# Gram squares of 64 and 32 tokens in separate column groups of TensorE, in the gated linear attention of a two-stack transformer

## The chip, the cores and the metric

The kernel runs on one core of a Trainium2 chip. The time is device microseconds of one execution, as the median of several. Engines: PE is TensorE (matmuls, with its weight loads PEld), DVE is VectorE, ACT is ScalarE, SP is SyncE and only issues transfers here.

## The reference

Two stacks of two layers each run over 256 tokens of width 1024. The first has, in every layer, attention, a gated linear attention (GLA), a convolution and a feed-forward part, for a latent and for a context stream; the second stack is another transformer behind it. The change touches only the GLA scan, which runs in both directions, over 4 heads with keys of 128 channels and values of 256:

```python
def step(s, inp):
    qc, kc, vc, gc = inp
    b = jnp.cumsum(gc, axis=2)
    rel = jnp.where(lower, b[:, :, :, None, :] - b[:, :, None, :, :], -jnp.inf)
    a = jnp.einsum('bhid,bhjd,bhijd->bhij', qc, kc, jnp.exp(rel))
    o = jnp.einsum('bhid,bhde->bhie', qc * jnp.exp(b), s) + jnp.einsum('bhij,bhje->bhie', a, vc)
    ...
```

The weight of key j for query i is a sum over channels of q, k and a decay that depends on the channel and on both tokens.

## The kernel before, in words

All activations lie channels first (128 partitions) by tokens. Weights come as a stream of 723 loads of 512 KB. ACT rounds each load to its high part (`w_hi`, L1078), DVE takes the low part (`w_lo`, L1692), and a product `dense` is 24 matmuls of 128x256 for 8 tiles of weights (three for each tile, L489 to L491). PE, ACT and DVE each run an instruction list written out by hand, in order, and wait for one another through semaphores.

The first stack is four passes (layer by stream). Three of them are full ones and call `gla`: the context pass of layer 0 (here **the first pass**, its grams from 166 to 279 us), the latent pass of layer 0 (**the second**, 896 to 976 us) and the latent pass of layer 1 (**the third**, 1719 to 1798 us).

The kernel makes the 256x256 weights `A` without the chunks of the reference. It takes the pairs of tokens apart by level: for `half` in 128, 64, 32, 16, 8, 4, 2, 1 the tokens are cut into blocks of 2 x half, and a level holds the pairs with one token in the left half of a block and the other in its right half. The decay of such a pair splits at the middle of the block, so that `DL` can hold, for every token, k or q times its own part of the decay, and one matmul of `DL` with itself gives the products (the gram). Two directions make two steps for each level, 16 steps, and step 16 is the diagonal, made of `KG` and `QG` and added twice. So `STEPS` is 17, and for step j:

- DVE (`gla`, loop from L2037) first multiplies the decays of step j-1 with k and q (`decay`, L2017 and L2018, which raises `lev_ready`), then takes the differences of step j (`differences`, L2002/L2003 or L2007/L2008), then puts the gram of step j-2 into `A` (`place`: a copy for steps 0 and 1, for the others two copies under a mask, L2033, one for each half of the tokens), and then does what the interleaved units need, a `w_lo` above all. In steps 8 to 11 come four more passes over 1024 columns for the states (L1957 or L1966).
- ACT takes the exponential (L1366), evacuates the unit of PE and makes a `w_hi`.
- PE first runs the units that fill this step (a `dense` in each; in the first pass also, in most steps, `ada`, which is 16 matmuls with only two moving columns, L539, and in steps 13 to 16 the units of the states, L571 and L580), then waits for `lev_ready` of step j and for `a_copied` of step j-2, and makes the gram of step j: steps 0 and 1 at L733, 2 to 15 at L739, and the diagonal at L746, which waits for `a_copied` of step 14.

The grams of steps 2 to 15 are whole squares of 128 tokens, for 2 halves of the tokens and 4 heads, although the mask keeps only blocks of 2 x half on the diagonal of the square. Then, when all is placed, PE multiplies `A` with the values (L759, and L763 for the state). An fp32 matmul shows as two records in the trace, each with a weight load of its own, so that a step's 8 matmuls are 16 records. The fp32r matmuls of `dense` (L489 to L491) show as one record each.

L625, which the prediction reads, makes sums over channels for several heads: matmuls of 32 output columns and 256 moving ones, each head in another group of 32 columns of the array.

Of the kernel before, what the change touches and what calls it, by code (L numbers as in the profile page):

```python
# [28 lines left out]
P = 128  # L29
# [15 lines left out]
LEVELS = (128, 64, 32, 16, 8, 4, 2, 1)  # L45
# [29 lines left out]
GROUP, GROUPS = 32, P // 32  # L75
# [147 lines left out]
def program(nc, stream, first_in, rows_in, crow_in, ada_in, xt_in, cvec_in, vec1_in, vec2_in, glr_in, a2_in, const1_in, const2_in, small2_in, mask_in, out):  # L223
# [5 lines left out]
    with ExitStack() as ctx:  # L229
# [58 lines left out]
        KG = view(arena, 16 * S, GH, S)  # L288
        QG = view(arena, 20 * S, GH, S)
        VG = view(arena, 24 * S, QT, GH * GDV)  # L290
        Z = view(arena, 32 * S, 2 * GH, S)
        DL = view(arena, 32 * S, 2, GH, S)
# [159 lines left out]
        def _(pe):  # L452
# [265 lines left out]
            def gla(l, s):  # L718
                fill = gla_steps(l, s)
                a0 = n.at("a_copied")  # L720
                for j in range(STEPS):
                    for u in fill[j]:
                        unit(l, s, u)
                    pair = [aux[2 * (j % 2)], aux[2 * (j % 2) + 1]]
                    if j < STEPS - 1:
                        pe.wait_ge(sems["lev_ready"], at.up("lev_ready"))
                    if j >= 2:

                        pe.wait_ge(sems["a_copied"], a0 + j - 1)
                    if j < 2:  # L730
                        ks, qs = (0, P) if j == 0 else (P, 0)
                        for h in range(GH):
                            mm = pe.matmul(pair[0][:, h * P:(h + 1) * P], DL[:, j % 2, h, ks:ks + P],  # L733
                                           DL[:, j % 2, h, qs:qs + P], start=True, stop=True)
                    elif j < STEPS - 1:
                        for kt in range(QT):
                            for h in range(GH):
                                part = DL[:, j % 2, h, kt * P:(kt + 1) * P]
                                mm = pe.matmul(pair[kt][:, h * P:(h + 1) * P], part, part, start=True, stop=True)  # L739
                    else:  # L740

                        for kt in range(QT):
                            for h in range(GH):
                                tok = slice(kt * P, (kt + 1) * P)
                                for rep in range(2):
                                    mm = pe.matmul(pair[kt][:, h * P:(h + 1) * P], KG[:, h, tok], QG[:, h, tok],  # L746
                                                   start=rep == 0, stop=rep == 1)
                    mm.then_inc(sems["gram_done"], 1)
                n.up("a_copied", STEPS)
                if s == LAT:  # L750
                    pe.wait_ge(sems["hat_ready"], at.up("hat_ready", 2))

                pe.wait_ge(sems["a_copied"], n.at("a_copied"))
                for h in range(GH):
                    o = bank()
                    for c in range(2):
                        e = h * GDV + c * P
                        for kt in range(QT):
                            mm = pe.matmul(o[:, c * S:(c + 1) * S], VG[:, kt, e:e + P], A[:, h, kt, :],  # L759
                                           start=kt == 0, stop=kt == QT - 1 and s == CTX)  # L760
                        if s == LAT:
                            for d in range(2):
                                mm = pe.matmul(o[:, c * S:(c + 1) * S], state[:, d, h, c * P:(c + 1) * P],  # L763
                                               HAT[:, h, d, :], start=False, stop=d == 1)
                    done(mm)
# [207 lines left out]
            for l in range(DEPTH):  # L973
# [31 lines left out]
                for tt in range(QT):  # L1005
                    mm = pe.matmul(o[:, tt * MH * MV:(tt + 1) * MH * MV], w2["ckv"][:, 0, tt * P:(tt + 1) * P], vcols,
                                   start=True, stop=True)
# [1642 lines left out]
```

## Time and profile before

| | |
|---|---|
| median of 3 runs | 3044.44 us (3039.38 to 3047.6) |
| the profiled execution | 3033.33 us, span 3031.6 us |
| granted TensorE clock, mean | 0.955 |
| PE / PEld busy | 94% / 90% of the span |
| DVE / ACT busy | 73% / 50% |
| HBM read | 447 MB, 148 GB/s |

The profiled execution is one run and took 11.1 us less than the median of the others. The span runs from its first to its last instruction. PE's busy share is that of overlapping records; how close PE is to its limit is read from the distance between starts.

### The profile page before, as it was taken

Reading aid. Unit: us, or ns where it says so; the run is one execution under the profiler, and the core shown is the slowest. Engines: PE = TensorE matmul, PEld = TensorE weight load, DVE = VectorE, ACT = ScalarE, POOL = GpSimd, SP = SyncE. Lnnn points to the kernel's source line nnn. Section 1 sums busy time; section 2 is a strip of 40 time slices with the busy share of each in tenths; the row PEclk is TensorE's granted clock in tenths of the full one; section 3 lists DMA queues with packets and bytes.
Section 4 is the critical chain, followed back from the end, with each engine's and each line's share of the span. In section 5 each row is a group of like instructions: output and inputs, shape, how many; then the busy total and the mean of one; then the engine's idle time right before and its main releaser. Section 6 shows DMA issues by size and latency. Waiting matters only on the chain.

```text
span 3031.6 us, 54592 instructions
## 1 busy us (share of the span) xinstructions
PE 2838.8 (94%) x21440; PEld 2716.1 (90%) x21440; DVE 2204.4 (73%) x3798; ACT 1514.1 (50%) x3111; POOL 0.2 (0%) x4
## 2 busy tenths in 40 slices
PE   8999999999999999999989998999999889997998
PEld 7999889899989889889989997888998779995998
DVE  6976777678889876867767898867666665566655
ACT  3644345454565335445564653454555455555554
POOL 0000000000000000000000000000000000000000
PEclk7999999999999989989999999999999899998999
DMA  7542444456742333447733423335553325541554
GB/s 265 157 160 94 146 133 153 152 176 222 232 137 91 105 124 127 143 169 236 232 117 118 143 76 118 111 125 179 166 183 117 105 81 187 185 140 52 160 185 153
DMA packets 123335, 451.45 MB, mean 149 GB/s; under 512 B 13744, under 2 KB 15792, under 8 KB 122464
## 3 DMA queue, kind: packets, MB, share of 16 engines
q1 hardware_dynamic: 108704, 393.30, 40.2%
q10 hardware_dynamic: 14400, 54.86, 5.3%
q8 instruction: 171, 2.80, 0.4%
q14 instruction: 60, 0.49, 0.1%
HBM read 447.05 MB, written 1.05 MB: 148 GB/s over the span
## 4 chain that ended last, share of the span: by engine, by line
PE 65%; DVE 22%; ACT 6%; DMA 4%; issue 2%; SPq 0%; ACTq 0%; DVEq 0%
PE lin L489 15%; PE lin L490 15%; PE lin L491 15%; DVE arena L1869 5%; DVE w_lo L1692 5%; DMA w_raw<-in_stream 3%; PE lin L539 3%; PE aux L604 2%; ACT w_hi L1078 2%; PE aux L739 1%; DVE rstd L1717 1%; PE aux L651 1%; PE aux L672 1%; PE aux L595 1%; PE lin L517 1%
## 5 line engine op out<-in xcount | busy, mean ns | idle before, releaser
L1692 DVE TENSOR_TENSOR w_lo<-w_raw,w_hi 128x1024 fp32r<-128x1024 f32 x722 | 875.2, 1220 | 321.3 <-ACT w_hi L1078 314.9
L489 PE MATMUL lin<-h_hi,w_hi 128*128 128x256 f32 x3456 | 997.3, 289 | 5.2 <-ACT arena L1346 2.9
L1078 ACT ACTIVATE w_hi<-w_raw 128x512 fp32r<-128x512 f32 x1446 | 828.7, 623 | 323.8 <-DMA w_raw<-in_stream 232.8
L490 PE MATMUL lin<-h_lo,w_hi 128*128 128x256 f32 x3456 | 985.7, 285 | 0.0
L491 PE MATMUL lin<-h_hi,w_lo 128*128 128x256 f32 x3456 | 985.4, 285 | 0.0
L489 PEld LDWEIGHTS lin<-h_hi,w_hi 128*128 128x128 f32 x3456 | 672.2, 195 | 9.9 <-ACT arena L1346 4.9
L490 PEld LDWEIGHTS lin<-h_lo,w_hi 128*128 128x128 f32 x3456 | 671.9, 194 | 0.5
L491 PEld LDWEIGHTS lin<-h_hi,w_lo 128*128 128x128 f32 x3456 | 671.1, 194 | 0.0
L489 PE MATMUL lin<-s_hi,w_hi 128*128 128x256 f32 x1520 | 450.6, 296 | 26.6 <-DVE s_lo L1778 23.2
L490 PE MATMUL lin<-s_lo,w_hi 128*128 128x256 f32 x1520 | 441.0, 290 | 0.0
L491 PE MATMUL lin<-s_hi,w_lo 128*128 128x256 f32 x1520 | 440.0, 289 | 0.0
L489 PEld LDWEIGHTS lin<-s_hi,w_hi 128*128 128x128 f32 x1520 | 302.4, 199 | 36.2 <-DVE s_lo L1778 28.0
L490 PEld LDWEIGHTS lin<-s_lo,w_hi 128*128 128x128 f32 x1520 | 303.2, 199 | 1.1 <-issue 0.5
L491 PEld LDWEIGHTS lin<-s_hi,w_lo 128*128 128x128 f32 x1520 | 302.9, 199 | 0.0
L1869 DVE SCALAR_TENSOR_TENSOR arena<-arena,vec 128x256 f32<-128x256 f32 x720 | 290.2, 475 | 0.0
L1795 DVE SCALAR_TENSOR_TENSOR X<-X,gate_buf 128x256 f32<-128x256 f32 x120 | 50.9, 425 | 142.1 <-ACT gate_buf L1238 56.9
L539 PEld LDWEIGHTS lin<-cvec,a_raw 128*128 128x128 f32 x928 | 116.5, 202 | 11.5 <-DMA a_raw<-in_ada 8.9
L539 PE MATMUL lin<-cvec,a_raw 128*128 128x2 f32 x928 | 114.5, 254 | 7.1 <-DMA a_raw<-in_ada 7.0
L1717 DVE RECIPROCAL rstd<-std 128x256 f32<-128x256 f32 (+1 forms) x34 | 59.5, 1751 | 83.8 <-ACT std L1107 83.8
L1224 ACT ACTIVATE gate_buf<-lin 128x256 f32<-128x256 f32 x110 | 41.7, 379 | 102.6 <-PE lin L491 86.3
L517 PE MATMUL lin<-w_hi,h_hi 128*128 128x256 f32 x320 | 90.8, 284 | 1.5 <-ACT arena L1313 1.5
L519 PE MATMUL lin<-w_lo,h_hi 128*128 128x256 f32 x320 | 90.6, 283 | 0.0
(278 smaller groups left out, 3858.9 us busy)
## 6 DMA issues: line engine op xcount, KB each, us to landing
w_raw<-in_stream SPq DMA_DIRECT2D x723, 512.0 KB, 3.5
a_raw<-in_ada ACTq DMA_DIRECT2D x58, 512.0 KB, 3.4
arena<-in_rows ACTq DMA_DIRECT2D x38, 512.0 KB, 5.1
arena<-in_first SPq DMA_DIRECT2D x2, 2048.0 KB, 19.6
X<-in_tokens SPq DMA_DIRECT2D x2, 1024.0 KB, 14.6
s_f<-in_ada SPq DMA_DIRECT2D x4, 512.0 KB, 10.3
arena<-in_ada SPq DMA_DIRECT2D x4, 512.0 KB, 17.2
arena<-in_const ACTq DMA_DIRECT2D x1, 1856.0 KB, 7.9
```

What stands on the lines that cost most here:

```text
L489: used(pe.matmul(o, whi, hi[:, k, :], start=k == 0, stop=False), first)
L490: pe.matmul(o, whi, lo[:, k, :], start=False, stop=False)
L491: mm = pe.matmul(o, wlo, hi[:, k, :], start=False, stop=k == kcs - 1)
L517: mm = pe.matmul(o[:, 0:2 * P], xhi, whi, start=k == 0, stop=False)
L519: pe.matmul(o[:, 0:2 * P], xhi, wlo, start=False, stop=False)
L539: mm = pe.matmul(o[:, 0:2], w[:, k, :], cvec[:, k, :], start=k == 0, stop=k == KC - 1)
L604: mm = pe.matmul(aux[1][:, 0:S], c1("mean1024"), squares[:, k, :], start=k == 0, stop=k == KC - 1)
L1078: act.activation(w_hi[:, slot, part], w_raw[:, raw, part], ACT.Copy).then_inc(sems["hi_ready"], 1)
L1692: dve.tensor_tensor(w_lo[:, m % SLOTS, :], w_raw[:, m % RAW, :], w_hi[:, m % SLOTS, :].bitcast(F32), ALU.subtract).then_inc(sems["lo_ready ...
L1717: step(dve.reciprocal(r, std[0:rows, slot, :]))
L1795: dve.scalar_tensor_tensor(x[:, c, :], x[:, c, :], alpha, gate_buf[:, c % 2, :], ALU.mult, ALU.add).then_inc(sems["r_ready"], 1)
L1869: dve.scalar_tensor_tensor(CV[:, c, :], YP[:, c, tap:tap + S], v1(l, "conv_w", c * TAPS + tap), CV[:, c, :], ALU.mult, ALU.add).then_inc(s ...
```

## The change

In steps 4 to 15 (levels 32 to 1) each square of 128 tokens is replaced by the squares on its diagonal: two of 64 tokens for level 32, four of 32 tokens for the levels below. A square of tokens b to b+w is written to partitions b to b+w of PSUM, so that the squares of one head lie in different column groups of PE. The diagonal, too, is made in squares of 32 tokens. The rest of the 128x128 area in PSUM is no longer written; the mask leaves it out, as before. Steps 0 to 3 stay.

```diff
                     elif j < STEPS - 1:
+                        w = max(2 * LEVELS[j // 2], GROUP)
                         for kt in range(QT):
                             for h in range(GH):
-                                part = DL[:, j % 2, h, kt * P:(kt + 1) * P]
-                                mm = pe.matmul(pair[kt][:, h * P:(h + 1) * P], part, part, start=True, stop=True)
+                                for b in range(0, P, w):
+                                    part = DL[:, j % 2, h, kt * P + b:kt * P + b + w]
+                                    mm = pe.matmul(pair[kt][b:b + w, h * P + b:h * P + b + w], part, part, start=True, stop=True)
                     else:
 
                         for kt in range(QT):
                             for h in range(GH):
-                                tok = slice(kt * P, (kt + 1) * P)
                                 for rep in range(2):
-                                    mm = pe.matmul(pair[kt][:, h * P:(h + 1) * P], KG[:, h, tok], QG[:, h, tok],
-                                                   start=rep == 0, stop=rep == 1)
+                                    for b in range(0, P, GROUP):
+                                        tok = slice(kt * P + b, kt * P + b + GROUP)
+                                        mm = pe.matmul(pair[kt][b:b + GROUP, h * P + b:h * P + b + GROUP], KG[:, h, tok], QG[:, h, tok],
+                                                       start=rep == 0, stop=rep == 1)
```

`P` is 128, `GROUP` 32, `QT` 2 halves of the tokens, `GH` 4 heads. The count of matmuls goes from 8 to 16 in steps 4 and 5, from 8 to 32 in steps 6 to 15, and from 16 to 64 in the diagonal. No other engine's list changes.

On PE at the end of the first pass's grams, steps 15 and 16 (L739, now L741, is the gram of a step; L571 and L580 belong to the states, L539 is `ada`), the difference is:

```order
 L491 MATMUL lin<-h_hi,w_lo 128x256
 L571 MATMUL lin<-const,s_f 128x128 x8
-L739 MATMUL aux<-arena 128x128 x8
+L741 MATMUL aux<-arena 32x32 x32
 L539 MATMUL lin<-cvec,a_raw 128x2 x8
 L580 MATMUL lin<-arena,s_f 128x256 x8
-L746 MATMUL aux<-arena 128x128 x16
-L759 MATMUL lin<-arena 128x256 x16
+L749 MATMUL aux<-arena 32x32 x64
+L762 MATMUL lin<-arena 128x256 x16
 L489 MATMUL lin<-h_hi,w_hi 128x256
```

Nothing moves past anything else: each gram stands where it stood, in more and smaller pieces (L759 and L762 are the same line).

On PE at the end of the second pass's grams, before:

```order
L491 MATMUL lin<-h_hi,w_lo 128x256
L739 MATMUL aux<-arena 128x128 x8
L746 MATMUL aux<-arena 128x128 x16
L759 MATMUL lin<-arena 128x256 x2
L763 MATMUL lin<-s_f,arena 128x256 x2
```

and now:

```order
L491 MATMUL lin<-h_hi,w_lo 128x256
L741 MATMUL aux<-arena 32x32 x32
L749 MATMUL aux<-arena 32x32 x64
L762 MATMUL lin<-arena 128x256 x2
L766 MATMUL lin<-s_f,arena 128x256 x2
```

Here the gram of step 15 and the diagonal follow each other with no unit between them: 24 matmuls have become 96.

## Rows read from the trace of the kernel before

**Rows 1.** page, part 1 (busy us, share of the span, instructions) and part 4 (chain)
```profile
PE 2838.8 (94%) x21440; PEld 2716.1 (90%) x21440; DVE 2204.4 (73%) x3798; ACT 1514.1 (50%) x3111; POOL 0.2 (0%) x4
...
PE 65%; DVE 22%; ACT 6%; DMA 4%; issue 2%; SPq 0%; ACTq 0%; DVEq 0%
```

**Rows 2.** groups of matmuls on PE: line, shape, count | busy us, mean ns | idle
```profile
L739 PE MATMUL aux<-arena 128*128 128x128 f32 x672 | 85.8, 282 | 4.7 <-DVE arena L2018 4.7
...
L746 PE MATMUL aux<-arena 128*128 128x128 f32 x96 | 11.2, 275 | 0.0
```

**Rows 3.** timeline, PE, one step of the first pass: start us, us, instructions, xcount
```profile
203.41 1.84 PE L539 MATMUL lin<-cvec,a_raw 128*128 128x2 f32 x16
205.11 2.03 PE L739 MATMUL aux<-arena 128*128 128x128 f32 x16
206.90 0.36 PE L489 MATMUL lin<-h_hi,w_hi 128*128 128x256 f32 x1
207.10 0.28 PE L490 MATMUL lin<-h_lo,w_hi 128*128 128x256 f32 x1
...
211.56 0.47 PE L739 MATMUL aux<-arena 128*128 128x128 f32 x2
```

**Rows 4.** timeline, PE, around four column groups in use (L625)
```profile
300.14 0.28 PE L490 MATMUL lin<-h_lo,w_hi 128*128 128x256 f32 x1
300.26 0.28 PE L491 MATMUL lin<-h_hi,w_lo 128*128 128x256 f32 x1
300.47 1.07 PE L625 MATMUL aux<-arena,const 128*32 128x256 f32 x16
301.47 0.39 PE L489 MATMUL lin<-h_hi,w_hi 128*128 128x256 f32 x1
301.69 0.28 PE L490 MATMUL lin<-h_lo,w_hi 128*128 128x256 f32 x1
```

**Rows 5.** instructions of L625 up to 300.6 us: first and last start
```profile
L625 PE MATMUL aux<-arena,const x4: 403/403/404, 300.5 to 300.5; 128*32 128x256 f32 x4
```

**Rows 6.** timeline, PE, the same shape over all 128 columns (L595)
```profile
1259.18 3.62 PE L595 MATMUL aux<-X,const 128*128 128x256 f32 x16
```

**Rows 7.** timeline, DVE, the decays that release the gram at 211.56
```profile
207.37 0.68 DVE L2018 TENSOR_TENSOR arena<-arena 128x512 f32<-128x512 f32 x1
```

**Rows 8.** busy us by stretch: PE, PEld, DVE, ACT, POOL, PEclk, DMA share, GB/s
```profile
220.00:235.00 15.00, 15.00 (x134) 15.00 (x132) 15.00 (x22) 7.20 (x14) 0.00 (x0) 1.00 0.55 175
905.00:965.00 60.00, 57.81 (x487) 56.85 (x486) 60.00 (x89) 30.59 (x50) 0.00 (x0) 1.00 0.33 106
```

**Rows 9.** timeline, DVE, one step of the second pass, from w_lo to w_lo
```profile
962.78 1.20 DVE L1692 TENSOR_TENSOR w_lo<-w_raw,w_hi 128x1024 fp32r<-128x1024 f32 x1
...
967.55 1.20 DVE L1692 TENSOR_TENSOR w_lo<-w_raw,w_hi 128x1024 fp32r<-128x1024 f32 x1
```

**Rows 10.** timeline, DVE, end of the second pass's grams
```profile
969.89 1.33 DVE L2033 COPY_PREDICATED arena<-masks,aux 128x512 f32<-128x512 uint8 x2
...
975.68 1.33 DVE L2033 COPY_PREDICATED arena<-masks,aux 128x512 f32<-128x512 uint8 x2 [2.22 <-PE aux L746]
```

**Rows 11.** timeline, PE, the same stretch
```profile
970.02 2.05 PE L739 MATMUL aux<-arena 128*128 128x128 f32 x16
971.91 3.74 PE L746 MATMUL aux<-arena 128*128 128x128 f32 x32
977.11 1.10 PE L759 MATMUL lin<-arena 128*128 128x256 f32 x4 [1.47 <-issue]
```

**Rows 12.** timeline, PE, first pass, a gram at the lower clock
```profile
188.42 1.84 PE L539 MATMUL lin<-cvec,a_raw 128*128 128x2 f32 x16
190.58 3.51 PE L739 MATMUL aux<-arena 128*128 128x128 f32 x16 [0.32 <-DVE arena L2018]
```

**Rows 13.** busy us by stretch, same columns as rows 8
```profile
190.90:194.30 3.40, 3.40 (x18) 3.40 (x17) 3.40 (x6) 1.06 (x1) 0.00 (x0) 0.50 0.44 157
```

**Rows 14.** page, part 3: the queue that fetches instructions
```profile
q8 instruction: 171, 2.80, 0.4%
```

## The prediction

> **What bounds the kernel now.** The page comes first: PE is busy 94% of the span and is 65% of the chain of waits, with DVE 22% [rows 1]. So work taken from PE counts, unless DVE stands right behind it. The groups of PE then say how large the edited part is: 672 records at L739 and 96 at L746 [rows 2], that is 14 steps of 16 and one of 32 in each of three passes. In the timeline of the first pass one gram runs from 205.11 to the next product at 206.90, 1.79 us for 16 records, 112 ns each [rows 3]. The edited part (12 steps and a diagonal of 3.57 us) is 25 us in a pass and 75 us in all. That is the most that could go.
>
> Whether it goes is read from the two kinds of passes. In the first, PE has `ada` beside `dense`, a step is 211.56 - 205.11 = 6.45 us [rows 3], and PE is the bound. In the second the table of busy time shows DVE busy 60.00 of 60 us while it makes the steps [rows 8], and DVE goes from one `w_lo` to the next in 967.55 - 962.78 = 4.77 us [rows 9]. There a faster gram only makes PE wait. The third pass repeats the second.
>
> **The price of a small square.** The trace has one place where groups of 32 columns are used in turn, L625. Its first four records start together [rows 5], and 16 records with 256 moving columns take 301.47 - 300.47 = 1.00 us [rows 4]. The same 16 records over all 128 columns take about 3.3 us, from 1259.18 to about 1262.45 (3.62 us to the modelled end less some 0.35) [rows 6]. So four column groups stream at once, a round of four in about 0.215 us. With 32 moving columns a round should take 32/256 of that, 27 ns; a step of 64 records is 16 rounds, 0.43 us. That is the lower bound. The upper bound is no overlap at all: 32 moving columns for each of 64 records, a quarter of 112 ns each, 1.79 us. I take **0.65 us**, near the lower end because the row shows the overlap, half as much again because no row shows weights of 32 columns renewed every 27 ns. For 64 tokens, two groups at once, 32 records are 16 rounds of 54 ns, 0.86 us; I take 0.90 (upper bound 1.79). For the diagonal, 32 rounds, 0.86 us; I take 1.3 (upper bound 3.57).
>
> **The price of changing over.** Into L625 the distance of starts is 300.47 - 300.26 = 0.21 instead of 0.12 us, and out of it 301.69 - 301.47 = 0.22 after 1.00 us of which the four rounds are 0.86 [rows 4]. Out of today's gram it is 207.10 - 206.90 = 0.20 [rows 3]. Going in costs 0.09 and coming out 0.14 + 0.02, so 0.25 us for each step. The Trainium skill, "TensorEngine Tiling (Array Packing)", Key Properties, says that a change of tiling mode drains the engine; by that rule, the trace agrees, with this 0.25 us.
>
> **First pass.** Steps 6 to 15: 1.79 - 0.25 - 0.65 = 0.89 us less, ten times, -8.9. Steps 4 and 5: 1.79 - 0.25 - 0.90 = 0.64, twice, -1.3. The diagonal: 3.57 - 0.25 - 1.3 = 2.0, -2.0. Together -12.2 us on PE.
>
> Three things give some of it back. DVE: its step is 4.8 us, and steps 8 to 11 each hold one more operation of about 1.1 us, 23.8 us for the four. PE would need 6.45 - 0.89 = 5.6 us for a step with `ada` and 3.9 for step 8, which has none (`ada` takes 205.11 - 203.41 = 1.70 [rows 3]), 20.7. DVE is already busy 15.00 of 15 us there [rows 8]. It has slack, since the decays for the gram at 211.56 ended at about 207.97 [rows 7], 3.6 us early, some 2.7 with the faster PE. The stretch and step 12, again without `ada`, use that up, and I put back 1.3 us. The clock: I allow for one more stretch at half clock than now, +1.7 us (below). Lost cover for the states' units (they wait for ACT with the gram as filler): within these. Sum of the first pass: **-9.2 us**.
>
> **Second and third pass.** In the steps nothing, hidden by DVE. The end differs: the last gram starts when its decays are ready, at 970.02, the diagonal at 971.91 [rows 11], and DVE, done with step 14 at about 971.2, waits for PE twice and places the diagonal at 975.68 [rows 10]. Now the gram of step 15 ends by 970.9, the diagonal may start once step 14 is placed, at 971.2, and takes 1.3 us and the changeover; with the 0.3 us from last start to DVE's start, the place comes at 972.9, 2.8 us earlier. Step 15 is placed meanwhile. A x V at 977.11 [rows 11] follows. ACT has activations of its own to finish first and cannot evacuate 2.8 us earlier, but four banks are free. Twice -2.8, of which I take off 0.6 for a colder start of A x V: **-5.0 us**.
>
> **Sum.** -14.2 us, on the profiled execution's 3033.3 a time of 3019. That execution lies 11 us under the median, so I set the change against the median: 3044.4 - 14.2 = 3030.2 us. DVE, ACT and the transfers get no work. Instructions grow by 608 matmuls and weight loads each in a pass, 3,648 in all; the queue that fetches them moves 2.80 MB in 0.4% of the DMA time today [rows 14], about 65 bytes for each of PE's 42,880, and gets 8% more. I cost that at nothing.
>
> **Rivals.**
>
> *The pieces cost by the record, not by their columns (0.12).* If small records don't overlap, a step is 1.79 + 0.25 us, 0.25 more than now. Twelve steps and the diagonal give +3 us in the first pass; in the others only the end grows, by 0.5 each. Then the time is 3044.4 + 4 = 3048. Against it speaks the common start of four records [rows 5]; for it, that those had 256 columns to stream. The Trainium skill speaks for it: the same page, Instruction Overhead, gives each matmul about 60 cycles and warns against tiling a dimension that is already small, as the moving one is here. At 2.4 GHz that would be 25 ns a record, 1.6 us for 64, 1.85 with the changeover, and no gain; no row here has such short records in different column groups.
>
> *The clock falls more often (0.18).* In the first pass the gram behind an `ada` began at 190.58 and took 3.51 us [rows 12], since the granted clock was 0.50, the 1.2 GHz level, from 190.9 to 194.3 [rows 13]. Before it PE had run 16 matmuls of two moving columns and then waited 0.32 us for DVE [rows 12]. The smaller gram lengthens each such thin stretch. A stretch of 3.4 us at half clock costs 1.7. If five of the eleven steps with `ada` bring one, four more than I allow, that is +6.8, and one at each end of the latent passes another +3: 3040 us. For it speaks that each step then has 2.9 us of dense work in 5.6; against it, that four groups streaming at once are not idle.
>
> *PE starves for instructions (0.14): the slower side.* A step of the second pass would issue 128 records for the gram (64 matmuls, 64 loads) and 48 for the `dense`, 176 in 4.78 us, and 208 in the first pass in 5.6. So the supply has to deliver one each 27 ns; there it decides. The trace shows 32 in 1.00 us (31 ns) only in a short burst [rows 4], and over long stretches 112 ns for a pair, 56 each [rows 3]. At 35 ns a step of the latent passes becomes 6.2 us, +1.4 ten times, and the diagonal 9.0, +5.4: +19 in each, +15 in the first pass, +54 in all, 3098 us. At 56 ns it is +195, 3239. Against it: PE is paced by the array in those stretches (112 ns for 128 columns twice), so they only bound the supply from one side.
>
> **How the numbers follow.** Forecast 0.53, the rivals 0.12, 0.18 and 0.14, and 0.03 that all goes better (lower bounds for every square, nothing given back, 3023). A difference of 0.3%, 9 us, is about what a measurement of this kernel can tell from none: faster ends at 3035.3, slower starts at 3053.6. The forecast lies below the first almost wholly, the clock's rival one time in three: faster 0.58. Most of the clock's rival, the rival by the record and a little of the forecast are within: 0.26. Starvation and the ends of the others: 0.16. The range takes in the first three cases with some 4 us for the median's scatter, 3018 to 3050, and leaves starvation out.
>
> **What would show it.** Records of a 32-token step starting within 0.5 to 0.8 us from first to last, four to a round; a distance of about 5.6 us between grams in the first pass where it was 6.45, unchanged 4.77 in the second, with PE now waiting for DVE (L2018) about 1 us before each gram; the diagonal placed some 2.8 us sooner after the last decays. Wrong would be: first-to-last over 1.5 us (by the record or starved, the latter if `dense` behind it slows too), or PEclk under 1.00 in the stretches from 195 to 270 us.

## The result, and the profile after

| | before | changed |
|---|---|---|
| median | 3041.58 us (7 runs, 3033.29 to 3056.62) | 3025.88 us (7 runs, 3022.54 to 3032.68) |
| ratio | | 0.9947, interval 0.9924 to 0.997 |
| the profiled execution | 3033.33 us | 3023.83 us, span 3022.1 us |
| mean granted clock | 0.955 | 0.952 |

The change saves 15.7 us by the medians, where 14.2 were forecast. The profiled executions differ by only 9.5 us, since that of the kernel before lies 8.2 us under its median; this is why the forecast was set against the median.

The page of the changed kernel, in the order of [rows 1] and [rows 14]:

```profile
PE 2807.6 (93%) x23264; PEld 2677.2 (89%) x23264; DVE 2203.6 (73%) x3798; ACT 1512.8 (50%) x3111; POOL 0.2 (0%) x4
...
q8 instruction: 185, 3.03, 0.4%
...
PE 61%; DVE 24%; DMA 6%; ACT 6%; issue 3%; SPq 0%; ACTq 0%; DVEq 0%
```

PE has 31 us less to do, which is more than the time fell, and part of the chain has gone from PE to DVE and to "issue". The groups of PE with shapes kept apart (busy us, mean ns | idle before), to be held against [rows 2]:

```profile
L741 PE MATMUL aux<-arena 128*32 128x32 f32 x1920 | 23.2, 200 | 20.9 <-DVE arena L2021 20.9
L741 PE MATMUL aux<-arena 128*64 128x64 f32 x192 | 7.5, 237 | 0.3 <-DVE arena L2021 0.3
L749 PE MATMUL aux<-arena 128*32 128x32 f32 x384 | 4.1, 198 | 2.8 <-issue 1.9 <-DVE arena L2036 1.0
```

The idle time before the 32-token grams, 20.9 us, is new (all grams of steps 2 to 15 had 4.7 [rows 2]): PE now waits for DVE's decays (L2021, which was L2018), and nearly all of it lies in the two latent passes. The timeline of PE in the first pass answers to [rows 3]:

```profile
205.10 1.84 PE L539 MATMUL lin<-cvec,a_raw 128*128 128x2 f32 x16
206.87 0.76 PE L741 MATMUL aux<-arena 128*32 128x32 f32 x64
207.56 0.39 PE L489 MATMUL lin<-h_hi,w_hi 128*128 128x256 f32 x1
207.79 0.28 PE L490 MATMUL lin<-h_lo,w_hi 128*128 128x256 f32 x1
...
210.63 0.76 PE L741 MATMUL aux<-arena 128*32 128x32 f32 x64
```

From the first record of the gram to the next product it is 207.56 - 206.87 = 0.69 us (1.79 before). The 64 starts lie within 0.57 us, in rounds of four that, but for the first, are 32 ns apart. The step behind it, without `ada`, is 210.63 - 206.87 = 3.76 us (4.74 before); those with `ada` are 5.45, 5.67 and 5.92 us (5.6 forecast, 6.45 before). In the second pass the same view shows the other case, and at its end something that was not foreseen:

```profile
956.67 0.77 PE L741 MATMUL aux<-arena 128*32 128x32 f32 x64 [0.96 <-DVE arena L2021]
957.36 0.39 PE L489 MATMUL lin<-h_hi,w_hi 128*128 128x256 f32 x1
...
961.45 0.77 PE L741 MATMUL aux<-arena 128*32 128x32 f32 x64 [0.96 <-DVE arena L2021]
962.72 1.28 PE L749 MATMUL aux<-arena 128*32 128x32 f32 x127 [0.50 <-DVE arena L2036]
965.85 0.22 PE L749 MATMUL aux<-arena 128*32 128x32 f32 x1 [1.85 <-issue]
967.54 2.05 PE L762 MATMUL lin<-arena 128*128 128x256 f32 x4 [1.47 <-DVE arena L2036]
```

The distance of steps stays at 961.45 - 956.67 = 4.78 us, that of DVE in [rows 9], and PE waits 0.96 us in each. The diagonal's 128 records would be through in 1.1 us, but 127 of them run and then PE stands for 1.85 us, and the profile shows no engine that releases it ("issue"). The third pass has no such stop (same view):

```profile
1786.69 0.76 PE L741 MATMUL aux<-arena 128*32 128x32 f32 x64 [0.93 <-DVE arena L2021]
1787.95 1.30 PE L749 MATMUL aux<-arena 128*32 128x32 f32 x128 [0.50 <-DVE arena L2036]
1790.92 1.10 PE L762 MATMUL lin<-arena 128*128 128x256 f32 x4 [1.67 <-issue]
```

From the last gram to A x V it took 7.09 us before [rows 11]; now it is 6.09 in the second pass and 4.23 in the third. Behind the stop, A x V itself is slower. The first `dense` record after it, in the kernel before:

```profile
990.82 0.47 PE L489 MATMUL lin<-h_hi,w_hi 128*128 128x256 f32 x1
```

and in the changed kernel:

```profile
984.24 0.47 PE L489 MATMUL lin<-h_hi,w_hi 128*128 128x256 f32 x1
```

That is 990.82 - 977.11 = 13.7 us before and 984.24 - 967.54 = 16.7 us now. Busy time by stretch (columns as in [rows 8]) for the two stretches of [rows 8], and three short ones, the last in A x V:

```profile
220.00:235.00 15.00, 14.59 (x287) 14.17 (x285) 15.00 (x22) 7.31 (x14) 0.00 (x0) 0.89 0.57 177
905.00:965.00 60.00, 48.29 (x1113) 45.26 (x1111) 59.03 (x88) 33.08 (x51) 0.00 (x0) 0.97 0.33 107
222.70:226.10 3.40, 3.40 (x45) 3.34 (x35) 3.40 (x6) 1.06 (x1) 0.00 (x0) 0.50 0.54 161
942.90:946.30 3.40, 3.40 (x35) 3.34 (x22) 3.40 (x5) 1.06 (x1) 0.00 (x0) 0.50 0.02 5
966.80:973.60 6.80, 6.06 (x14) 4.88 (x15) 6.80 (x18) 3.09 (x3) 0.00 (x0) 0.50 0.01 2
```

PE's busy time in the 60 us of the second pass fell from 57.81 to 48.29 with nothing gained there, and both stretches now hold time at the lower clock, 1.2 GHz, where both had 1.00.

What a stretch at half clock costs depends on where it falls. The one at 942.9 falls where DVE is the bound:

```profile
942.31 0.80 PE L741 MATMUL aux<-arena 128*32 128x32 f32 x64 [2.08 <-DVE arena L2021]
947.53 0.76 PE L741 MATMUL aux<-arena 128*32 128x32 f32 x64
951.88 0.76 PE L741 MATMUL aux<-arena 128*32 128x32 f32 x64 [0.52 <-DVE arena L2021]
```

The step that holds it takes 5.22 us and the next one 4.35, together 9.57, which is two steps of DVE's 4.78. PE made up the loss out of its own waits: the stretch cost no time. Nor did the one at 1762.1 in the third pass (steps of 4.80 us), nor the one at 222.7 in the first, where the gram behind it starts at 232.92 and DVE's decays for it end at 232.86. Where PE is the bound it does cost: 3.0 us for the 6.8 us in A x V, and 1.5 us for a stretch at 253.4 in the first pass (a step of 7.92 us, which is 6.43 in e6_fill below, where no such stretch falls in it).

From the first gram to the first `dense` behind A x V, the second pass took 94.99 us before and takes 96.62 now; the third took 94.20 and takes 91.40.

### The profile page after: what moved, and what is told of

Its sections match the earlier page's. It is cut to its first block, busy times and chain, and to the rows that moved or that the text cites. A ratio compares the mean times of both kernels' runs of the same rounds, so it can differ in the third digit from the quotient of the medians.

```text
span 3022.1 us, 58240 instructions
## 1 busy us (share of the span) xinstructions
PE 2807.6 (93%) x23264; PEld 2677.2 (89%) x23264; DVE 2203.6 (73%) x3798; ACT 1512.8 (50%) x3111; POOL 0.2 (0%) x4
## 3 DMA queue, kind: packets, MB, share of 16 engines
q8 instruction: 185, 3.03, 0.4%
## 4 chain that ended last, share of the span: by engine, by line
PE 61%; DVE 24%; DMA 6%; ACT 6%; issue 3%; SPq 0%; ACTq 0%; DVEq 0%
PE lin L489 14%; PE lin L490 14%; PE lin L491 14%; DVE w_lo L1695 5%; DVE arena L1872 5%; DMA w_raw<-in_stream 4%; PE lin L539 2%; ACT w_hi L1081 2%; PE aux L604 2%; DVE rstd L1720 1%; DVE arena L2036 1%; PE aux L651 1%; PE aux L672 1%; DMA a_raw<-in_ada 1%; PE aux L595 1%
## 5 line engine op out<-in xcount | busy, mean ns | idle before, releaser
L539 PEld LDWEIGHTS lin<-cvec,a_raw 128*128 128x128 f32 x928 | 116.5, 202 | 13.5 <-DMA a_raw<-in_ada 10.7
L539 PE MATMUL lin<-cvec,a_raw 128*128 128x2 f32 x928 | 115.0, 255 | 8.8 <-DMA a_raw<-in_ada 8.8
```

The costliest lines, as they stand in the source:

```text
L539: mm = pe.matmul(o[:, 0:2], w[:, k, :], cvec[:, k, :], start=k == 0, stop=k == KC - 1)
```

## Experiments

Twelve kernels ran, each beside runs of the kernel before on the same chip. Two figures help beyond the median. Every run has its span and its mean granted clock c. The time at half clock is 2(1 - c) times the span, and **span times c** is the length the run would have if PE's work alone filled it and the clock never fell. Where PE waits for DVE that condition fails: a stretch of 3.4 us at half clock as at 942.9 lengthens nothing, but takes 1.7 us off span times c. Such a stretch is called free below. Single runs of the kernel before have a standard deviation of about 5 us in the span and 4 in span times c. Means over the runs, with their standard errors (e3_one_group, e5_group_major and e13_shifted ran once each and stand in their own sections):

| kernel | runs | median us | ratio, interval | span x c | at half clock |
|---|---|---|---|---|---|
| before (beside e1, e2, e3, e5) | 18 | 3038.70 | | 2895.6 ± 0.7 | 284 ± 3 |
| changed, as above | 7 | 3025.88 | 0.9947, 0.9924 to 0.997 | 2876.7 ± 1.1 | 297 ± 5 |
| e1_context | 7 | 3029.63 | 0.9958, 0.994 to 0.9977 | 2882.8 ± 1.4 | 290 ± 4 |
| e2_latent | 12 | 3043.18 | 1.0008, 0.9991 to 1.0024 | 2889.4 ± 1.0 | 302 ± 4 |
| before (beside e6, e7) | 17 | 3038.13 | | 2895.6 ± 0.9 | 282 ± 3 |
| e6_fill | 6 | 3019.34 | 0.9942, 0.9929 to 0.9955 | 2881.5 ± 1.5 | 273 ± 4 |
| e7_whole_less_dve | 10 | 3034.16 | 0.999, 0.9974 to 1.0006 | 2891.0 ± 0.8 | 286 ± 4 |
| e7_small_less_dve | 4 | 3010.86 | 0.9908, 0.989 to 0.9926 | 2866.7 ± 3.0 | 284 ± 7 |
| before (beside e9 to e12) | 26 | 3040.63 | | 2895.5 ± 0.8 | 287 ± 2 |
| e9_latent_fill | 12 | 3031.83 | 0.9972, 0.9959 to 0.9985 | 2888.0 ± 1.0 | 284 ± 4 |
| e10_fill_from_6 | 6 | 3021.71 | 0.9936, 0.9915 to 0.9956 | 2878.0 ± 0.5 | 285 ± 4 |
| e11_changed_again | 9 | 3018.86 | 0.9937, 0.9918 to 0.9957 | 2874.2 ± 0.9 | 292 ± 5 |
| e12_before_fill | 12 | 3038.26 | 0.9997, 0.9985 to 1.0009 | 2894.1 ± 0.9 | 287 ± 3 |

### Where the gain is made: the first pass, or the latent ones

Small squares in the context pass alone, or in the latent passes alone (`s == LAT`):

```diff
-                        w = max(2 * LEVELS[j // 2], GROUP)
+                        w = max(2 * LEVELS[j // 2], GROUP) if s == CTX else P
...
+                                w = GROUP if s == CTX else P
-                                    for b in range(0, P, GROUP):
+                                    for b in range(0, P, w):
```

> Small squares only in the first (context) pass, whole squares in the two latent passes. Theory A (PE bounds the first pass, DVE the steps of the latent ones): the first pass is as short as with the whole change, 104 to 106 us from its first gram to A x V instead of 114.2, and the time is 9 to 12 us below the kernel before, about two thirds of the change. Rival B (the gain is spread evenly over the three passes): 5 us below. Rival C (the half-clock stretches that small squares bring cost more in the latent passes than their ends give): at or below the time of the whole change, 14 us or more under the kernel before.

> Small squares only in the two latent passes. Theory A: the steps stay at 4.77 to 4.9 us and the diagonal is placed 2.8 us sooner, so each latent pass is 1.4 to 3 us shorter from first gram to A x V, and the time is 3 to 6 us below the kernel before. Rival B (evenly spread): 10 us below. Rival C: no gain or slower, because A x V starts at half clock (the changed kernel's profile has it so in the second pass) and loses 3 us behind the grams.

The first has a ratio of 0.9958, 9.1 us less by the medians and 12.8 by span times c, 11.1 without the free stretch that its first pass has like the changed kernel's. Its first pass takes 106.09 us to A x V, 0.1 above what theory A allows, with 3.4 us more at half clock in it than the changed kernel has there. So theory A holds and the larger part of the gain is made here.

The second has 1.0008, where theory A expected 3 to 6 us less. Within the passes theory A holds: they take 79.74 and 78.40 us to A x V where the kernel before has 81.29 and 80.50. By span times c it saved 6.2 us. It also spent 18 ± 5 us more at half clock, and the mean span is 2.7 ± 2.0 us longer. The two savings by span times c, 12.8 and 6.2, add up to 19.0, and the changed kernel has 18.9 and, in its second set of runs, 21.3.

Two stretches of the latent passes' half clock in e2_latent (columns as above), the second in A x V:

```profile
947.10:950.50 3.40, 3.40 (x67) 3.34 (x54) 3.40 (x6) 1.06 (x1) 0.00 (x0) 0.50 0.07 28
977.80:981.20 3.40, 3.05 (x7) 2.52 (x8) 3.40 (x10) 2.51 (x3) 0.00 (x0) 0.50 0.02 5
```

The first is free: the step that holds it takes 5.90 us, and 5.91 in the kernel before. So is one at 1773.1. The second costs 1.5 us: A x V takes 15.23 us to the first `dense` behind it instead of 13.70. Without the two free ones, span times c gives the latent passes 2.8 us and not 6.2. To that `dense` the second pass takes 94.97 us, nothing gained on 94.99, because the stop and the slow A x V take back what the end of the grams gives; the third takes 92.10 after 94.20. Why the mean of the whole kernel is not some 2 us shorter, as these passes are, the runs don't show.

### What makes a small square cheap: one column group, or a poor order

All squares written to partitions 0 up, so that they share one column group; the weights `A` are then incomplete:

```diff
-                                    mm = pe.matmul(pair[kt][b:b + w, h * P + b:h * P + b + w], part, part, start=True, stop=True)
+                                    mm = pe.matmul(pair[kt][0:w, h * P + b:h * P + b + w], part, part, start=True, stop=True)
```

The diagonal, too, goes to partitions 0 to 31, and its two additions to a square follow each other directly.

> The small squares all go to partitions 0 up, so to the same column group of PE, one behind the other; the rest of the squares is left out of the result. Theory A (the column groups work side by side): 64 records of 32 columns take 64 times 27 ns, 1.7 us, from first to last start instead of 0.57, the 32 records of 64 columns the same, the diagonal 3.4, and the first pass is as long as before or up to 4 us longer (114 to 118 us). Rival D (small squares are cheap because they are small, or because records are issued every 8 ns whatever group they go to): 0.57 us again, first pass 105 us.

And the same squares, where they belong, but in steps 4 to 15 all squares of a column group first, then those of the next:

```diff
-                        for kt in range(QT):
-                            for h in range(GH):
-                                for b in range(0, P, w):
+                        for b in range(0, P, w):
+                            for kt in range(QT):
+                                for h in range(GH):
```

> The same squares, but all eight of one column group first, then all of the next, so that neighbours in the instruction list share a group (steps 4 to 15; the diagonal stays). Theory A1 (PE starts records in the order of the list, apart from waiting for its group): no overlap but at the borders, 64 records take 1.6 to 1.75 us. Theory A2 (a record that waits for its group lets those for other groups past): with enough records looked at ahead it stays at 0.6 to 0.9 us. First pass 105 us under A2, 113 to 116 under A1.

Timeline of PE, first pass, of the kernel with one column group:

```profile
204.85 1.84 PE L539 MATMUL lin<-cvec,a_raw 128*128 128x2 f32 x16
206.63 2.21 PE L741 MATMUL aux<-arena 128*32 128x32 f32 x64
208.77 0.39 PE L489 MATMUL lin<-h_hi,w_hi 128*128 128x256 f32 x1
```

and of the one in order of groups:

```profile
208.03 1.91 PE L741 MATMUL aux<-arena 128*32 128x32 f32 x64
```

With one group a gram takes 208.77 - 206.63 = 2.14 us, more than the whole squares' 1.79: its records start 32 ns apart. In order of groups the 64 starts span 1.72 us; they are 32 ns apart too, and only some 6 records at each border between groups overlap. In the changed kernel the same 64 take 0.57. The squares are the same in all three; what differs is that in the changed kernel each matmul goes to another column group than the one ahead of it. The first pass takes 127.32 us to A x V with one group, more than the 114 to 118 expected: a record took 32 ns and not 27, and 27 us of the pass were at half clock, where the kernel before has 10. In order of groups it takes 116.24, as theory A1 has it. Executions: 3054.60 and 3043.11 us, one run each, beside a median of 3038.70: neither is a gain.

### What bounds the latent steps

DVE puts only the first half of each gram of steps 2 to 16 into `A` in the latent passes, in the kernel before (whole squares) and in the changed one (small squares). The other half of `A` is left out.

```diff
-                    for kt in range(QT):
+                    for kt in range(QT if s == CTX else 1):
                         ins = dve.copy_predicated(A[:, :, kt, kt * P:(kt + 1) * P], over(masks[:, j - 2, :], GH),
```

> The kernel before (whole squares), but in the latent passes DVE puts only one half of each gram of steps 2 to 16 into A: the other half of A is left out, and DVE has 0.66 us less in each step. Theory D (the latent steps of the changed kernel are bound by DVE, those of the kernel before by PE and DVE almost equally): here PE is the bound, 4.66 to 4.75 us a step, as the first pass's steps without ada have 4.74; hat steps fall from 5.9 to about 5.3. Rival E (something else paces the steps, such as the loads or the chain of ACT's exponential): 4.77 as before.

> The changed kernel (small squares) with the same part left out: DVE puts only one half of each gram of steps 2 to 16 into A in the latent passes. Theory D: the bound moves to DVE at 4.1 to 4.2 us a step (PE needs 3.8), so ten steps and the end give some 6 to 8 us a pass, and this kernel is 12 to 18 us faster in the latent passes than the one with whole squares and the same part left out, on top of the 10 to 13 us of the first pass: ratio to before 0.985 to 0.990. Rival E: the steps stay at 4.7 to 4.8 and the gap between the two kernels is that of the changed kernel and the one before, 16 us.

PE's timeline late in the second pass, the kernel before (the next gram is at 970.02 [rows 11]):

```profile
965.24 2.05 PE L739 MATMUL aux<-arena 128*128 128x128 f32 x16
```

whole squares with less work on DVE:

```profile
961.45 1.95 PE L739 MATMUL aux<-arena 128*128 128x128 f32 x16
966.11 1.95 PE L739 MATMUL aux<-arena 128*128 128x128 f32 x16
```

and small ones with less work on DVE:

```profile
948.81 0.76 PE L741 MATMUL aux<-arena 128*32 128x32 f32 x64 [0.33 <-DVE arena L2021]
952.98 0.76 PE L741 MATMUL aux<-arena 128*32 128x32 f32 x64 [0.34 <-DVE arena L2021]
```

The late steps of the kernel before take 4.78 us, at DVE's pace. With 0.66 us less on DVE the whole squares take 4.66, only 0.12 less, and PE waits for nothing: that is PE's own bound. (The kernel before has 4.66 as well between its grams at 910.88 and 929.52, while DVE, which is ahead there, goes on at 4.78.) With small squares the step falls to 4.17, and even then PE waits for DVE. So theory D holds for the steps. In sum: from first gram to A x V the small squares save 5.5 and 8.9 us in the two latent passes of this pair (78.21 to 72.73, 79.00 to 70.11), where the changed kernel saves 1.4 and 2.8. The pair differs by 23 us in the medians (3034.16 and 3010.86); at least 22 were expected. The ratio of 0.9908 lies just outside the 0.985 to 0.990 expected, and the second pass of this kernel has a stop too, as below.

### Is it given back at the lower clock

PE's waits in the latent passes are filled with useless matmuls, ahead of the wait for `lev_ready` and ahead of the one before A x V:

```diff
+                    if s == LAT and 4 <= j < STEPS - 1:
+                        pe.wait_ge(sems["a_copied"], a0 + j - 1)
+                        for _ in range(4 if j in (10, 11) else 2):
+                            pe.matmul(pair[0][:, 0:S], c1("mean1024"), const1[:, 0:S], start=True, stop=True)
...
+                    if s == LAT and h == 0:
+                        for _ in range(4):
+                            pe.matmul(o[:, 0:S], c1("mean1024"), const1[:, 0:S], start=True, stop=True)
```

> The changed kernel, with PE's waits of the two latent passes filled: before each gram of steps 4 to 15 it runs 2 matmuls of 128x256 (4 in steps 10 and 11) into the PSUM area that the gram then overwrites, and 4 before A x V, all of them useless. Each shows as 2 records of 0.216 us, 0.43 us in all. Theory G (in the latent passes the smaller squares did gain 1.4 to 2.8 us a pass, and it is given back because PE's new waits of 1 us bring more stretches at half clock): distances of steps stay at 4.79, no stretch at half clock inside the latent gram passes (the changed kernel has four, at 942.9, 966.8, 1714.3 and 1762.1), A x V 6 us behind the last gram at full clock, time about 3021, ratio to before 0.992 to 0.994. Rival H (stretches at half clock come from elsewhere, or the total is set by their chance places): the time stays at the changed kernel's 3026, ratio 0.995. Rival I (the filling is itself in the way): distances of steps over 4.9 and a time of 3030 or more.

> Small squares in the two latent passes only, as in e2_latent, with PE's waits filled from step 6 on (2 useless matmuls of 128x256 before each gram, 4 in steps 10 and 11, 4 before A x V). Steps 4 and 5, where the filling of e6_fill lengthened steps of 4.75 and 4.19 us to 5.62 and 5.02, are left alone. Theory G (the 1.5 to 2.8 us gained in each latent pass are given back by stretches at half clock that PE's new waits bring): ratio to before 0.998 to 0.999, -3 to -6 us, where e2_latent had 1.0008; no half-clock stretch within the latent gram passes. Rival H (what is gained there is lost by chance elsewhere, or was never gained): ratio as e2_latent's, 1.000 to 1.001.

> The changed kernel with the same filling, in the latent passes from step 6 on. Theory G: 1.5 us faster than e6_fill for the steps 4 and 5, 3 to 6 us faster than the changed kernel, that is 3016 to 3020 where the kernel before has 3038; ratio 0.9935 to 0.994. Rival H: as the changed kernel's run beside it.

> The changed kernel once more, on the same chip as the filled ones: ratio to before 0.9947 with some 0.001 to either side; half the half-clock time above e10_fill_from_6 is what the filling saves.

> The kernel before (whole squares), filled where it has waits in the latent passes: 2 useless matmuls in steps 10 and 11, 3 before A x V. Theory G: little to win, because whole squares leave PE no waits in the other steps and its latent passes hold no half-clock stretch: ratio 0.999 to 1.000. Rival J (filling before A x V helps any version): ratio 0.998 or less, and then the gain of the filled kernels is no return of what the small squares lost.

Ten us of the second pass in the changed kernel (columns as above):

```profile
938.00:948.00 10.00, 7.92 (x161) 7.51 (x161) 10.00 (x15) 3.48 (x7) 0.00 (x0) 0.83 0.27 77
```

and with the filling, e6_fill:

```profile
938.00:948.00 10.00, 9.90 (x188) 8.93 (x187) 10.00 (x15) 3.83 (x6) 0.00 (x0) 1.00 0.22 81
```

In the latent passes' grams of the filled kernels' profiles no half clock is left but the one at the first gram, which the kernel before has too (e10_fill_from_6 has one more, at its A x V). For small squares in the latent passes alone, filling turns 1.0008 into 0.9972, and the intervals don't meet (the two ran on different chips, each against the kernel before on its own): the time at half clock falls from 302 to 284 us, that of the kernel before. The kernel before gains nothing by it (0.9997), so rival J falls. The filling is worth something in that pair, more than the 3 to 6 us that theory G expected. But the cause that theory G gives is not shown: the half clock that went from the steps had been free. The profiles place 3.5 us of the gain in the two passes (94.97 to 92.07 and 92.10 to 91.47 us, to the first `dense` behind A x V), most of it the stop of the next section and the slow A x V behind it, which e9_latent_fill doesn't have. Where the rest was gained is open.

For the changed kernel the total is as rival H has it: 0.9936 filled and 0.9937 not. Span times c is 3.8 us longer with the filling, and free stretches explain it: e11_changed_again has two in its latent steps (942.3 and 1761.5) and e10_fill_from_6 none, which makes 3.4 us of difference in span times c and none in time. e6_fill (0.9942, the upper edge of what theory G expected) is 4.8 us longer by this figure than the first set of the changed kernel: 3.4 for the free stretches and 3.4 for its filled steps 4 and 5 (5.62 and 5.02 us where they had 4.75 and 4.19, 1.7 in each pass), less 1.9 for the stop that it doesn't have. No version is shown to beat the changed kernel.

### The stop before the last record of the diagonal

The 1.85 us stop recurs before the same record in e11_changed_again, e7_small_less_dve and (1.33 us) e5_group_major, and elsewhere inside the diagonal of e2_latent and e10_fill_from_6, always in the second pass; e6_fill and e9_latent_fill have none. Traffic of the changed kernel's queues from 963.0 to 964.7 us (packets, MB, share):

```profile
q8 instruction: 1, 0.02, 4.5%
```

One block of instructions (3.03 MB in 185 packets is 16.4 KB each) is being fetched; it starts at 963.39, ends at 964.61, and PE goes on at 965.85. In all six the fetch starts between 0.9 us ahead of the last record that PE still starts and 0.1 us after it, and PE goes on 1.2 to 1.4 us after it has ended. To move the place where a block ends, 50 matmuls of 32x32 were added in the waits of steps 14 and 15 (j = 13 and 14) of the second pass:

```diff
+                    if l == 0 and s == LAT and j in (13, 14):
+                        pe.wait_ge(sems["a_copied"], a0 + j - 1)
+                        for k in range(25):
+                            b = k % 4 * GROUP
+                            pe.matmul(pair[0][b:b + GROUP, b:b + GROUP], const1[:, 0:GROUP], const1[:, 0:GROUP], start=True, stop=True)
```

> The changed kernel with 50 useless matmuls of 32x32 (100 records and 100 weight loads) in PE's waits of steps 14 and 15 of the second pass alone, so that the place where the instruction queue's next block of 16 KB is needed falls some 200 instructions away. Theory K (the 1.85 us for which PE stood still before the last record of the second pass's diagonal, with an instruction fetch under way, is one block of instructions that came too late, because the last gram and the diagonal use more than a block's worth in 3 us): no stall inside the diagonal, from the first record of the last gram to A x V 4.2 us as in the third pass, where the changed kernel had 6.09 in the second. Rival L (something at this place of the program holds PE, such as ACT's table load or the placing of the last gram): 6.1 us again. The time itself cannot show it.

Timeline of PE:

```profile
959.95 0.76 PE L746 MATMUL aux<-arena 128*32 128x32 f32 x64 [0.96 <-DVE arena L2026]
961.22 1.30 PE L754 MATMUL aux<-arena 128*32 128x32 f32 x128 [0.50 <-DVE arena L2041]
964.17 1.10 PE L767 MATMUL lin<-arena 128*128 128x256 f32 x4 [1.66 <-issue]
```

All 128 records run, and A x V comes 4.22 us behind the last gram instead of 6.09. The block's fetch now starts at 962.33, when the diagonal's last record starts, and falls into PE's wait for A x V. Rival L falls, since the place in the program is the same. That the useless matmuls also fill two waits is not the reason either: e10_fill_from_6 has those waits filled and stops all the same. So theory K holds: the stop is an instruction block that comes too late. Each kernel shows it in one profiled execution (two for the changed squares).

What follows the stop costs time as well. The five kernels that stood for 1.8 to 2.2 us all have half clock in the A x V right behind it (from 966.8, 966.2, 977.8, 961.8 and 967.3 us), e5_group_major with 1.33 us has none there, and no latent pass without a stop has any. In e13_shifted the second pass takes 91.45 us from its first gram to the first `dense` behind A x V, where the changed kernel takes 96.62: 1.9 of the 5.2 us are the stop, 3.0 the slow A x V, 0.3 lie at the first gram. One execution of each is compared here, two of the changed kernel (96.62 and 96.76). (The run took 3015.67 us and the kernel before beside it 3033.80, with 271 and 273 us at half clock; one run each, too few to show 5 us in the time.)

## Why the prediction was right, and where it was not

**The bound.** As forecast: in the latent passes DVE takes 4.77 us a step and PE's own step is only 0.1 us shorter, and PE was the bound in the first pass. Both e7 kernels show the one, e1_context the other.

**Price of a small square.** 0.57 us for the burst of 32-token squares (0.65 forecast), 0.93 for the 64-token ones (0.90), 1.10 for the diagonal (1.3). Changing over: 0.69 - 0.57 = 0.12 us from the last start, then 207.79 - 207.56 = 0.23 for the first product instead of 0.12, and 0.09 going in: with the burst 0.89 us for a gram (0.90 forecast). One term was missed: the whole square, too, had 0.20 instead of 0.12 behind it [rows 3], so that a step saves 0.98 and not 0.89. Ten steps without that 0.09 are 0.9 us too few.

**First pass.** -9.2 us forecast; from its first gram to A x V it is 104.62 us after 114.21, -9.6. The mechanism is right and three sizes were off, in part against each other. PE saved an estimated 13.3 and not 12.2: 0.98 us ten times, and 0.2 more in the diagonal. The steps that DVE paces gave back the rest, about 2.2, where 1.3 was put; steps 8 to 11 come at DVE's 5.9 us each, as the forecast's 23.8 us for four has it. The clock took 1.5 us (the stretch at 253.4) where 1.7 was allowed.

**Latent passes.** -5.0 us forecast, twice -2.8 less 0.6 for a cold A x V. To A x V the third pass is as forecast, 7.09 - 4.23 = 2.86 us, and to the first `dense` behind it 94.20 - 91.40 = 2.8. The second lost what it gained and is 96.62 - 94.99 = 1.6 us longer: 1.9 us went into the stop and 3.0 into the A x V at half clock behind it. Together -1.2 us where -5.0 were forecast. The steps at fault are "I cost that at nothing", of the instructions, and the 0.6 us allowed for the cold A x V, which measured 3.0. "In the steps nothing, hidden by DVE" holds: the new waits cost nothing, and the half clock that came with them was free.

**The sum.** The passes of the profiled execution are 9.6 + 1.2 = 10.8 us shorter and not 14.2. By the medians the change is worth 15.7 us in the first set of runs and 22 in the second (18.7 ± 2.6 by the mean spans). Span times c gives 19 and 21 us; three free stretches (222.7, 942.9, 1762.1), if they fall in every execution as in both profiled ones, account for 5.1 of that, and 14 to 16 us are left. The passes of the profile, less what the clock cost in them (1.5 and 3.0), give 15.3. So 14 to 16 us is the worth of the change at full clock; the forecast has 16.5 for it, its terms without the 1.7 and 0.6 for the clock. That the first median lies within 1.5 us of the forecast is partly luck: the latent passes gave 4 us less than forecast, and the clock's scatter, some 12 us in the time at half clock of a single run and so 6 in its time, is as large as such an error.

**The rivals.** *By the record*: fell. It needs 1.79 us for 64 records; they took 0.57, 9 ns each. It is right where the squares share a column group, or come in the order of groups: 32 ns a record. The Trainium skill, "TensorEngine Tiling (Array Packing)", Instruction Overhead, gives about 60 cycles for each matmul, an estimate of 25 ns at 2.4 GHz: the traces come near it in one column group (32 ns) and not over four in turn (9 ns). *The clock falls more often*: half right. Its sign came, PEclk 0.89 in 220:235, and the changed kernel's profile has five more stretches in the gram passes than before (222.7, 253.4, 942.9, 1762.1, and 966.8 in A x V). But three of them were free, and the other two cost 1.5 and 3.0 us: 2.2 beyond the 2.3 allowed, where the rival named 9.8. *Starved of instructions*: as a steady rate it fell. 128 instructions in 0.57 us are 4.5 ns each, where it needed 27 to decide. As an event it was real, once in a run: 1.9 us long, and with the half clock behind it 4.9. The forecast's nothing looked at the queue's mean traffic [rows 14], not at the 384 instructions of the last gram and the diagonal, which use up one and a half blocks (of some 250) in 2.4 us.

## What to carry to other kernels

Cut a block-diagonal matmul into squares on separate column groups, and write the list so that each matmul goes to another group than the one ahead of it; in the order of groups the pieces cost as much as the whole. Before counting what PE saves, see how far the next engine is behind in each stage. Look also at what the many small instructions draw from the instruction queue in the densest burst, not on average. A fall of the clock is priced by the stage it falls in: where another engine sets the pace, compare the distances of steps before and after, since it may cost nothing. In a kernel whose clock changes by chance, compare span times mean clock as well as the median, but take off the free stretches first: here they made 5 of 19 to 21 us.

## What the runs showed of the hardware

- fp32 records of 32 weight columns and 32 moving columns start 32 ns apart while they stay in one column group, and about 9 ns apart on average over four groups in turn. A following record of another group starts early only if it is near in the list: some 6 records overlapped at each border of groups.
- PE issued 64 matmuls and 64 weight loads in 0.57 us, 4.5 ns for each.
- Instructions came in blocks of 16 KB, and PE went on 1.2 to 1.4 us after the end of a fetch that it was waiting for (six kernels). With bursts this dense a stop depends on where in the list a block ends: 50 useless matmuls ahead of the burst took it away.
- After the stops of 1.8 to 2.2 us inside the diagonal, the granted clock was 0.50 for 3.4 or 6.8 us in A x V behind it (five kernels of five); A x V took 16.7 us instead of 13.7 for 6.8 us of it.
- A stretch of 3.4 us at half clock in steps that DVE paces cost nothing (5.22 + 4.35 us for two steps of 4.78); where PE was the bound it cost 1.5 us.
- Filling waits of 1 us with useless matmuls kept the granted clock at 1.00 through the latent grams behind the first. In one kernel it went with a gain of 0.36% (1.0008 to 0.9972), in the changed one with none.
